# Selected and banded attention of a decoder step: values as stationary operand in two column halves, probabilities scaled on POOL, masks added by TensorE

## What is computed

```python
# selected branch (16 blocks of 64 keys are chosen, and the prompt has 16: so all keys up to the query's own)
mask = kpos <= qpos
# banded branch
mask = (d >= 0) & (d <= 512)                 # d = qpos - kpos
# both
s = q @ k.T * 64 ** -0.5
p = exp(s - max(s)); p = p / p.sum(-1)       # over the keys that the mask leaves
o = p @ v
...
o = gate_cmp * o_cmp + gate_slc * o_slc + gate_win * o_win   # sigmoid gates, per head and query
```

## Time and profile before

| | |
|---|---|
| time, median of 3 runs | 2466.98 us (2466.42 to 2467.43) |
| the profiled execution, its own time | 2464.73 us |
| its span, first to last instruction | 2463.1 us |
| busy in the span: PE, PEld | 2299.4 us (93%), 2130.6 us (86%) |
| busy in the span: DVE, ACT, POOL | 1154.1 us (47%), 802.2 us (33%), 285.3 us (12%) |
| mean granted clock of TensorE (1.0 is 2.4 GHz) | 0.967 |
| the stage of the change | 754.3 to 1036.4 us |

### The profile page before, as it was taken

One profiled execution on the slowest core, in us unless ns is written; L12 is line 12 of the kernel. 1 busy time (PEld: TensorE's weight loads), 2 busy tenths in 40 slices (PEclk: granted clock), 3 DMA queues, 4 the chain that ended last, 5 costly groups with the idle time before them and its releaser, 6 DMA issues. The chain is left out here.

```text
span 2463.1 us, 39913 instructions
## 1 busy us (share of the span) xinstructions
PE 2299.4 (93%) x15431; PEld 2130.6 (86%) x15431; DVE 1154.1 (47%) x2060; ACT 802.2 (33%) x1795; POOL 285.3 (12%) x549
## 2 busy tenths in 40 slices
PE   6998798999877999857999999999999999999999
PEld 6977798999766899834899999878999999999997
DVE  4547766312758877634422233335333443333335
ACT  5355364444345666423312122213211111111110
POOL 1004221003203422244000000000000000000000
PEclk9999699999998999988999999999999999999999
DMA  5011442321110000176112132211111111111111
GB/s 155 27 35 44 144 129 86 109 103 35 45 37 1 1 2 18 48 235 211 42 49 52 39 86 52 86 48 52 52 52 52 35 52 52 35 52 52 35 35 69
DMA packets 177129, 156.73 MB, mean 64 GB/s; under 512 B 24770, under 2 KB 158069, under 8 KB 176884
## 3 DMA queue, kind: packets, MB, share of 16 engines
q1 hardware_dynamic: 158660, 120.37, 16.7%
q0 software_dynamic: 7136, 19.07, 2.6%
q10 hardware_dynamic: 11152, 14.80, 1.8%
HBM read 142.76 MB, written 15.59 MB: 64 GB/s over the span
## 5 line engine op out<-in xcount | busy, mean ns | idle before, releaser
L181 PE MATMUL ps<-brT_r,ff_wih 128*128 128x344 f32 x1008 | 322.4, 320 | 0.0
L183 PE MATMUL ps<-brT_r,ff_wi_r 128*128 128x344 f32 x1008 | 322.0, 319 | 0.0
L182 PE MATMUL ps<-xnT_r,ff_wih 128*128 128x344 f32 x1008 | 321.8, 319 | 0.0
L3935 ACT ACTIVATE ff_sa<-ps 128x344 f32<-128x344 f32 x66 | 30.2, 458 | 563.5 <-PE ps L183 563.5
L181 PEld LDWEIGHTS ps<-brT_r,ff_wih 128*128 128x128 f32 x1008 | 189.9, 188 | 1.0
L183 PEld LDWEIGHTS ps<-brT_r,ff_wi_r 128*128 128x128 f32 x1008 | 189.7, 188 | 0.0
L181 PE MATMUL ps<-x_r,mg_wh 128*128 128x344 f32 x576 | 185.2, 321 | 4.7 <-DVE xnT_r L169 4.7
L182 PEld LDWEIGHTS ps<-xnT_r,ff_wih 128*128 128x128 f32 x1008 | 189.1, 188 | 0.4
L182 PE MATMUL ps<-xnT_r,mg_wh 128*128 128x344 f32 x576 | 184.5, 320 | 0.0
L3971 DVE TENSOR_TENSOR x<-x,ps 128x512 f32<-128x512 f32 (+1 forms) x198 | 134.9, 686 | 100.9 <-PE ps L183 100.1
L183 PE MATMUL ps<-x_r,mg_w_r 128*128 128x344 f32 x552 | 176.4, 320 | 0.0
(11 more groups left out here) (667 smaller groups left out, 5625.7 us busy)
## 6 DMA issues: line engine op xcount, KB each, us to landing
ff_wi<-in_w_ffn_in SPq DMA_DIRECT2D x42, 512.0 KB, 5.1
mg_w<-in_w_in SPq DMA_DIRECT2D x23, 512.0 KB, 4.1
ff_wo<-in_w_ffn_out SPq DMA_DIRECT2D x11, 1024.0 KB, 4.9
s_pages<-in_cache_kv_slc SPq DMA_DIRECT2D x64, 128.0 KB, 4.7
s_pages<-in_cache_kv_slc POOLq DMA_DIRECT2D x64, 128.0 KB, 3.1
sc_X<-in_cache_kv_cmp SPq DMA_DIRECT2D x56, 128.0 KB
sc_X<-in_cache_kv_cmp POOLq DMA_DIRECT2D x56, 128.0 KB, 2.4
mg_w<-in_w_branch SPq DMA_DIRECT2D x23, 256.0 KB, 4.5
```

Source lines behind the costliest of these rows:

```text
L181: nc.tensor.matmul(out, wh, xh, start=(first and k == 0), stop=False)
L182: nc.tensor.matmul(out, wh, xl, start=False, stop=False)
L183: ins = nc.tensor.matmul(out, wl, xh, start=False, stop=(last and k == n - 1))
L3935: nc.scalar.activation(sa[:, s % 2, :], ps[:, s % 2, 0:BLK], ACT.Silu).then_inc(silued, 1)
```

## The change

Units are put in another order, in **groups** of four: two neighbouring heads in the selected branch, then the same two in the banded branch. Then, for each unit:

- The masks are added by PE, between the two halves of a score product: a matmul of minus the identity with the mask table (`future` for the last block, `past` for the first block of the band), 128 columns, fp32r.
- DVE only takes the minimum, and the reciprocal of the row sums (`share`). Its order is `maximum(u + 3)`, `share(u + 1)`, copies of unit u.
- POOL multiplies the whole tile `p` in place with two factors per row, the reciprocal and the gate (`tensor_scalar`, two multiplications).
- PE's order is `scores(u + 2)`, `products(u - 1)`, and for odd u `attend((u - 3) / 2)`, which takes two units at once. In it the 64 value columns are the stationary operand and `pT` streams past. The first head's result goes to PSUM partitions 0 to 63, the second's to 64 to 127, so that it comes out turned. All of a group adds up in one PSUM tile, which begins with a product that turns `acc`. DVE copies it to `brT` once for a group (`out`). `use` and `turn_out` are gone.
- `p` and `pT` have four places instead of two.

The diff, cut to its core:

```diff
-    units = [(i, h, br) for i in range(QT) for h in range(H) for br in range(2)]
+    units = [(i, 2 * a + hh, br) for i in range(QT) for a in range(H // 2) for br in range(2) for hh in range(2)]
...
                         nc.tensor.matmul(out, qA[:, i % 2, h, :], kk, start=True, stop=False)
+                        if a + n == hi - lo:
+                            nc.tensor.matmul(out[:, (n - 1) * P:n * P], minus_one[:, :], future[:, :],
+                                             start=False, stop=False)
+                        if a == 0 and br == 1 and i >= 4:
+                            nc.tensor.matmul(out[:, 0:P], minus_one[:, :], past[:, :], start=False, stop=False)
                         ins = nc.tensor.matmul(out, qB[:, i % 2, h, :], kk, start=False, stop=True)
...
                 def products(u):
-                    pe.wait_ge(exped, u + 1)
+                    pe.wait_ge(normed, u + 1)
...
+                def attend(k):
+                    i, h, br = units[2 * k]
+                    g, out = h // HPG, ps[:, 6 + k // 2 % 2, 0:P]
+                    wait_kept(pe, first_item[2 * k + 2])
+                    if br == 0:
+                        if k >= 4:
+                            pe.wait_ge(okept, k // 2 - 1)
+                        nc.tensor.matmul(out, acc[:, h // 2, i * P:(i + 1) * P], c("ident"), start=True, stop=False)
+                    lo, hi = keys(2 * k)
                     for b in range(hi - lo):
-                        kv = kvsw[:, lo + b, br * 256 + g * 128:br * 256 + (g + 1) * 128]
-                        ins = nc.tensor.matmul(ps[:, 6 + u % 2, 0:P], pT[:, u % 2, b * P:(b + 1) * P],
-                                               kv, start=(b == 0), stop=(b == hi - lo - 1))
+                        v = kvsw[:, lo + b, br * 256 + g * 128 + HD:br * 256 + (g + 1) * 128]
+                        for hh in range(2):
+                            ins = nc.tensor.matmul(out[hh * HD:(hh + 1) * HD, :], v,
+                                                   part(pT_all, 2 * k + hh)[:, b * P:(b + 1) * P],
+                                                   start=False, stop=(br == 1 and b == hi - lo - 1))
...
-                for u in range(NU):
+                for u in range(NU + 1):
                     if u + 2 < NU:
                         scores(u + 2)
-                    products(u)
                     if u >= 1:
-                        attend(u - 1)
+                        products(u - 1)
+                    if u >= 3 and u % 2:
+                        attend((u - 3) // 2)
...
             def _(pool):
-                    pool.wait_ge(exped, u + 1)
-                    pchain.link(pool, nc.gpsimd.tensor_tensor(f[:, k:k + 1], sm[:, k:k + 1], minus[:, :], ALU.pow))
-                    nc.gpsimd.tensor_tensor(f[:, k:k + 1], f[:, k:k + 1], gate, ALU.mult).then_inc(shared, 1)
+                    pool.wait_ge(shared, u + 1)
+                    p = part(p_all, u)[:, 0:(hi - lo) * P]
+                    nc.gpsimd.tensor_scalar(p, p, f[:, k:k + 1], gate, ALU.mult, ALU.mult).then_inc(normed, 1)
...
             def _(dve):
-                    if br == 1 and i >= 4:
-                        chain.link(dve, nc.vector.tensor_tensor(s[:, 0:P], s[:, 0:P], c("band"), ALU.subtract))
-                    chain.link(dve, nc.vector.tensor_tensor(s[:, n - P:n], s[:, n - P:n], c("causal"),
-                                                            ALU.subtract))
                     nc.vector.tensor_reduce(mx[:, u % 4:u % 4 + 1], s[:, 0:n], AX.X, ALU.min).then_inc(maxed, 1)
+                def share(u):
+                    dve.wait_ge(exped, u + 1)
+                    nc.vector.reciprocal(f[:, u % 4:u % 4 + 1], sm[:, u % 4:u % 4 + 1]).then_inc(shared, 1)
+                def out(e):
+                    dve.wait_ge(attended, 2 * e + 2)
+                    nc.vector.tensor_copy(brT[:, h // 2, i * P:(i + 1) * P], ps[:, 6 + e % 2, 0:P]).then_inc(okept, 1)
...
                 for u in range(NU):
-                    if u + 2 < NU:
-                        maximum(u + 2)
+                    if u + 3 < NU:
+                        maximum(u + 3)
+                    if u + 1 < NU:
+                        share(u + 1)
                     for m in range(first_item[u], first_item[u + 1]):
                         keep(nc.vector, m, u)
-                    if u >= 1:
-                        use(u - 1)
+                    if u >= 5 and u % 4 == 1:
+                        out((u - 5) // 4)
```

More of the change, by code:

```diff
@@ L1911, in stage_slc_win, with part @@
                   for n in range(2))
-        p_ = st.sb("p", [P, 2, S])
-        pT = st.sb("pT", [P, 2, S])
+        SW = 5 * P
+        p_all = st.sb("p", [P, 2 * (S + SW)])
+        pT_all = st.sb("pT", [P, 2 * (S + SW)])
+        def part(x, u):
+            _, h, br = units[u]
+            lo = 2 * S * br + (SW if br else S) * (h % 2)
+            return x[:, lo:lo + (SW if br else S)]
         mx = st.sb("mx", [P, 4])
@@ L1917, in stage_slc_win @@
         sem = st.sem
[L1918 to L1923, removed]
+        shared = sem("shared")
+        minus_one, future, past = (st.sb(n, [P, P], FR) for n in ("minus_one", "future", "past"))
+        tables = sem("tables")
+        zeroed, qkept, scored, maxed, exped, normed, pturned, pkept_a, pkept_v, attended, okept = (
+            sem(n) for n in ("zeroed", "qkept", "scored", "maxed", "exped", "normed", "pturned", "pkept_a", "pkept_v",
+                             "attended", "okept"))
         def wait_kept(eng, m):
@@ L2003, in products @@
                             ins = nc.tensor.transpose(ps[:, 4 + m % 2, b * P:(b + 1) * P],
-                                                      p_[:, u % 2, (a + b) * P:(a + b + 1) * P], c("ident"))
+                                                      part(p_all, u)[:, (a + b) * P:(a + b + 1) * P], c("ident"))
                         ins.then_inc(pturned, 1)
[L2007 to L2015, removed]
-                    for b in range(hi - lo):
-                        kv = kvsw[:, lo + b, br * 256 + g * 128:br * 256 + (g + 1) * 128]
-                        ins = nc.tensor.matmul(ps[:, 6 + u % 2, 0:P], pT[:, u % 2, b * P:(b + 1) * P],
-                                               kv, start=(b == 0), stop=(b == hi - lo - 1))
-                    ins.then_inc(attended, 1)
@@ L2032, in _ @@
                 turn_q(0)
                 turn_q(1)
+                pe.wait_ge(tables, 3)
                 scores(0)
                 scores(1)
-                for u in range(NU):
+                for u in range(NU + 1):
                     if u + 2 < NU:
                         scores(u + 2)
-                    products(u)
                     if u >= 1:
-                        attend(u - 1)
-                        if u % (2 * H) == 1 and u > 2 * H:
-                            turn_out(u // (2 * H) - 1)
@@ L2044, in _ @@
-                attend(NU - 1)
-                turn_out(QT - 1)
+                        products(u - 1)
+                    if u >= 3 and u % 2:
+                        attend((u - 3) // 2)
+                attend(NU // 2 - 1)
             @block.gpsimd
             def _(pool):
-                pchain.link(pool, nc.gpsimd.memset(minus[:, :], -1.0))
                 for u in range(NU):
@@ L2053, in _ @@
                     k = u % 4
-                    pool.wait_ge(exped, u + 1)
-                    if u >= 4:
-                        pool.wait_ge(used, u - 3)
+                    pool.wait_ge(shared, u + 1)
                     gate = gk[:, i, (1 + br) * H + h:(1 + br) * H + h + 1]
-                    pchain.link(pool, nc.gpsimd.tensor_tensor(f[:, k:k + 1], sm[:, k:k + 1], minus[:, :], ALU.pow))
-                    nc.gpsimd.tensor_tensor(f[:, k:k + 1], f[:, k:k + 1], gate, ALU.mult).then_inc(shared, 1)
+                    lo, hi = keys(u)
+                    p = part(p_all, u)[:, 0:(hi - lo) * P]
+                    nc.gpsimd.tensor_scalar(p, p, f[:, k:k + 1], gate, ALU.mult, ALU.mult).then_inc(normed, 1)
             @block.scalar
             def _(act):
[L2063 to L2066, removed]
+                for table, name, sign in ((minus_one, "ident", -1.0), (future, "causal", 1.0), (past, "band", 1.0)):
+                    nc.scalar.activation(table[:, :], c(name), ACT.Copy, scale=sign).then_inc(tables, 1)
                 for m in range(2):
@@ L2084, in _ @@
                 exponentials(0)
+                exponentials(1)
                 for u in range(NU):
[L2086 to L2090, removed]
+                    if u + 2 < NU:
+                        exponentials(u + 2)
                     for m in range(first_item[u], first_item[u + 1]):
                         keep(nc.scalar, m, u)
-                out(act, QT - 1)
             @block.vector
```

37 lines of the change are left out of this document (10 added, 27 removed).

## The result

The changed kernel takes 2497.27 us (median of 4 runs, 2493.9 to 2498.12), the kernel before 2466.7 beside it (4 runs, 2465.74 to 2467.43): a ratio of 1.0122 with a 95% interval of 1.0109 to 1.0136. It is slower, as forecast, by 30.6 us where 22 were expected, and inside the range.

What follows compares the result with a forecast made beforehand. The prediction took PE to bound the stage in tiles 4 to 7. Changes of +6.9 there, +12.7 in tiles 1 to 3 and +1.9 in tile 0 gave +21.5 on 2464.73; with 2.25 for the median, 2489 us (2466 to 2535).

Steps and rivals of the forecast that it cites:

- two waits a group: PE's turns without an attend: waits of 2.46 to 2.49 us in sum a group in tiles 4 to 7.
- 142.8 + 39.7: Tiles 4 to 7: PE's own work plus its waits in 16 groups, 182.5 us against 175.6 before.
- The prices hold: PE in the old tiles 4 to 7: prices per operation sum to 169.2 of the 175.6 us measured.
- changes of width: PE switching between full width and column halves around each attend: 0.24 us an attend, 0.48 a group.
- 0.59 + 0.82 + 1.35: Wait chain of a selected unit at n = 8: fixed delays, DVE's minimum and POOL's pass, in us.
- 0.55 + 0.70: PE's transposes and scores covering part of a selected unit's wait at n = 8, in us.
- 0.50 + 0.106: POOL's pass: fixed us plus us a block, 1.03 for 5 blocks and 1.35 for 8.
- the 0.69 and 1.01 us at which the sign turned: POOL's pass for 5 and 8 blocks: below these lengths the change would come out faster.
- by column: Rival on POOL's pass: 3.2 ns a column, 0.19 + 0.41 us a block, 2549 us in all; chance 0.09.
- line rate: Rival on POOL's pass: 0.19 + 0.106 us a block, as a copy's, 2469 us in all; chance 0.10.
- the halves don't overlap: Rival on PE's attend: column halves run without overlap, 58 us more over 32 groups, 2547 us; chance 0.05.
- 4 x (7.43 + 8.80): Tiles 2 and 3: four groups a tile, at 7.43 and 8.80 us a group including two waits.

Runs made afterwards that it cites:

- the first experiment: Changed kernel with DVE's reciprocal of unit u + 1 moved ahead of the minimum of u + 3: 2451.5 us, 0.9951 of the kernel before.
- the second experiment: Changed kernel with POOL's scaling split into two passes: 2735.26 us with one factor each, 2549.91 us with 1.0 as second factor in each.

## Why the prediction was right, and which terms were off

**The mechanism.** The forecast put the loss into two waits a group, where a turn has no attend, on minimum, reciprocal and POOL's pass. The waits are there, and they go when the reciprocal is moved: 184.3 to 159.9 us. The size came out by luck, as the terms show.

**Tiles 4 to 7: 182.5 forecast, 184.3 measured, by two errors that cancel.** "142.8 + 39.7" is 159.9 + 24.4 by the first experiment.

- *PE's work, 17.1 too low.* The step that failed is "The prices hold": 6.4 us of the old 175.6 were left over and not carried into the new sum. Half of them, 3.2 us, PE stood idle (172.44 of 175.60 in the earlier trace rows); the rest held the first passes of scores, priced at 0.23 by the later ones of the earlier trace rows: the pass that starts there at 1011.56 comes 0.31 after the first. This is the row of before (timeline of PE), which the prediction did not read:

```profile
1011.25 0.48 PE L1983 MATMUL ps<-x_r,a_q_r 128*128 128x512 f32 x1
```

  Masks at 0.12 instead of 0.06 add to it, and PE's waits around the turns of queries, 3.1 + 2.5 us. In tile 7 the scores of a group are 2 x 0.25 + 2 x 0.15 = 0.8 above the prices; over 16 groups 12.8, and with the 5.6 of the waits, less 1.0 for the cheaper changes of width, 17.4, against 17.1 to be explained (an estimate, since the smaller n are taken as tile 7).
- *The waits, 15.3 too high,* 1.5 a group and not 2.46 to 2.49. In the turn shown, the chain from 1042.29 to 1044.74 takes 2.45 us, forecast 0.59 + 0.82 + 1.35 = 2.76: the pass is 0.16 shorter, PE resumes after 0.06 and not 0.17. And PE's own work in the meantime, 1.43 us (1042.29 to 1043.72), was put at 0.55 + 0.70: the dearer scores cover more.

**POOL's pass** came out at 0.34 + 0.107 a block, forecast 0.50 + 0.106, above the 0.69 and 1.01 us at which the sign turned (0.874 and 1.194). By the prediction's own sum, 0.16 less on 64 waits takes 10 us off, so with the right pass it would have said 2479: PE's dearer work made up for it. And the reading behind it failed: the 0.607 us of the earlier trace rows for one factor holds a fixed part of 0.28 and not 0.50. It is 0.28 + 0.32 a block, as 602 ns for 128 columns and the further widths of the second experiment show, so "by column" was the better reading of that row, and the two-factor form does not follow it. The rule of the Trainium skill's "GPSIMD Engine Reference" (section 4.1, Engine selection), roughly line rate for one-input work, agrees with the slope of the two-factor pass, 0.83 ns as the copy's, and not with that of one factor, 2.5 ns; the fixed part, 0.34, lies midway between the 0.19 that the rival "line rate" took and the forecast's 0.50.

**Halves and changes of width.** 0.055 us a record, as forecast, and 0.21 an attend, forecast 0.24; "the halves don't overlap" is out. The loss that the Trainium skill's "TensorE: Matmul & The Clock Gate" (Part 3, Measured speedup vs the span model) has at three column tiles does not show at two halves.

**Tiles 0 to 3.** Tiles 2 and 3 were forecast at 4 x (7.43 + 8.80) = 64.9 us and took 64.7, again by two errors that cancel: without the waits they take 54.5, where the forecast had 45.0 of work, so the waits cost 10.2 and not 19.8. Tile 1 was forecast at 24.2 and took 30.5, the largest miss that nothing cancels: a low clock in a tile that had run at 1.00 was not in the sum. With the clock back the tile took 25.6 us. Tile 0 was forecast at 24.6 and took 26.9.

## What to carry to other kernels

In a strict queue a short instruction that others wait for belongs ahead of a long one that waits itself: here two exchanged calls are worth 43 us, more than the 30.6 that the whole change lost. When a sum of prices leaves a few per cent of the measured time over, these belong into the forecast too; here they held the dearer first pass behind each change of kind, and waits. And a mask of 128 columns took 0.11 to 0.12 us of PE here, twice its columns: price a short matmul with weights of its own from the distance of starts, not by its columns.

## What the runs showed of the hardware

- On POOL a multiplication of fp32 by two per-row factors in place takes 0.34 us + 0.107 a block of 128 columns, by one factor 0.28 + 0.320; with 1.0 as second factor 0.26 + 0.107. The form with less arithmetic takes three times as long a column.
- PE's waits on POOL in tile 1 (8 times, 2.8 us in sum, 0.7 at most) go with a granted clock of 0.68, and idle transposes in the turns of tiles 0 and 1 with 1.00; without the waits it was 0.82 to 0.93.
